# Key and block compression of the last mixer beside the feed-forward ahead of it, and the last pair's splits in another order

## The chip, the cores and the metric

One core of a Trainium2 chip runs the whole network for one sequence of 256 tokens in one launch. The metric is the device time of the launch in microseconds (us); lower is better. Three runs of a kernel give a median and its spread, and one more execution is recorded by the hardware profiler.

## The reference

Two blocks of two layers each, in float32, with 1024 features. The first block has a gated linear recurrence, an attention with a position bias, and a SwiGLU feed-forward behind each. The second block has a short convolution, shared keys and values, and a sparse attention with three branches, between four SwiGLU feed-forwards. What matters here is the last mixer, cut to its core:

```
def _compress(x_raw, pos, w1, b1, w2):          # 15 overlapping blocks of 32 tokens
    blocks = x_raw[:, :, idx] + pos
    return jax.nn.gelu(flat(blocks) @ w1 + b1) @ w2

k_cmp = _rmsnorm(_compress(kv[0], ...), k_norm[0]);  v_cmp = _compress(kv[1], ...)
k_sel = _rmsnorm(kv[2], k_norm[1]);  k_win = _rmsnorm(kv[4], k_norm[2])

def _nsa(x, ...):                                # 16 heads of 64, 4 groups of keys
    q = _rmsnorm(proj[..., :1024], q_norm);  gate = sigmoid(proj[..., 1024:])
    p_cmp = softmax(q @ k_cmp / 8, valid) * valid
    out = gate0 * (p_cmp @ v_cmp) + gate1 * attend(q, k_sel, v_sel) + gate2 * attend(q, k_win, v_win)
    return out @ w_o

def _swiglu(x, w_gate_up, w_down):
    a, b = jnp.split(x @ w_gate_up, 2, axis=-1)
    return (jax.nn.silu(a) * b) @ w_down
```

With 256 tokens every block is selected and the window covers all keys, so both of the other branches are plain causal attention. The shared keys and values come from the state after `ffn3`; the queries come from the state after `ffn4`.

## The kernel before

The phases are hgrn, ffn0, moba, ffn1, final, ffn2, conv, ffn3, kv, ffn4, nsa, ffn5. Each engine's instructions are written out by hand in one function per phase and engine; semaphores join them. Every weight is streamed in chunks of 1 MB (128 partitions x 2048 floats) through three buffers `raw` (`RING`). A float32 product of full accuracy is made of three fast ones: ACT copies the chunk to a rounded high part `whi`, DVE subtracts to get the low part `wlo` (both are called a split, `split`, L668 and L1200), and PE adds high x high, low x high and high x low.

SP issues the loads in the order of `Chunks.plan`. A load into a buffer waits until the chunk that held it, three earlier, was split by both engines; a chunk that is used unsplit (`direct`, the four `w1` of the compression) frees its buffer only when PE has multiplied with it.

A feed-forward (`ffn`) goes over 11 pairs of 256 hidden columns. For pair i there is a gate chunk g, an up chunk u and a down chunk d. PE's order per stage is g(i+1), then d(i), then u(i+1) (`across_pair` L1831 and L1833, `down_part` L1946). DVE's order is split g(i+1), `sum_gate(i)`, split d(i), `multiply(i)` (L1269, L1271), `low_part(i)` (L1286), split u(i+1); ACT has split g, `activate`, split d, `up_low` (L750), `high_part` (L756), split u. PE waits for `hlo_ready` of pair i before d(i). The last pair is made in two halves: `last_multiply`, `last_low` (L1282) on DVE, and `down_last` on PE, which adds the last down chunk first for token tile 0, then for tile 1. DVE's `add` (L1295) puts the sums into h, a root on GpSimd and `normalise` (L1222) follow, and PE's `turn` (L1889) transposes the result for the next phase.

The last mixer (`nsa`) does the following before its attention, in PE's order: projection of queries (two halves x two tiles, `along` L1848, L1849, L1854), gates (L2264, L2265), transposes of the normalised keys (L2280), compression with four direct chunks (L2293), key output (L2303), transposes of the queries (L2313), scores against the compressed keys (L2323), value output (L2330), 16 filler matmuls that compute nothing (`keep_warm` L1882), transposes of the compressed probabilities (L2337). DVE makes the squares and scales of keys and queries; the inverse roots come from GpSimd (`pow`, L1154).

Its attention handles 16 units: 8 pairs of heads, two branches each. For unit i, PE makes masked scores (L2120, L2124), DVE their maxima (L1490) and a scaling of these four values (L1494), ACT the exponentials with sums (L931), DVE the normalised probabilities (L1500 to L1508), PE the transposes (L2134), ACT the copy of these to SBUF (L939), PE the product with the values (L2356 with the compressed values, L2361 with the others), ACT and DVE the high and low part of the result once a pair (L944 `y_high`, L1513 `y_low`). Three of the four `out` chunks are split before the attention, the fourth after.

## Time and profile before

| | us |
|---|---|
| median of 3 runs | 1676.4 |
| lowest, highest | 1675.95, 1678.55 |
| profiled execution, its own time | 1678.77 |
| span of the profiled execution | 1677.0 |
| PE busy | 1653.9 |
| DVE busy | 1019.3 |
| ACT busy | 791.2 |
| mean granted TensorE clock | 0.995 |

The span runs from the first to the last instruction of the profiled execution. Busy times are sums per engine over the span; matmuls overlap in the array, so an engine at 99% may still hold short gaps between the starts of its instructions. The clock is a share of the full 2.4 GHz.

### The profile page before, as it was taken

What the parts mean: (1) busy time and instruction counts of PE and PEld (TensorE: products, weight loads), DVE (VectorE), ACT (ScalarE), POOL (GpSimd) and SP (SyncE); (2) the same over time, 40 slices, a digit from 0 to 9 for tenths busy, and PEclk for the clock granted to TensorE, in tenths of its full rate; (3) what the DMA queues carried; (4) which work ended last, traced back from release to release, by engine and by line L of the source; (5) the groups of instructions that cost most, each with busy time, mean ns of one, the idle gap of its engine ahead of it and who ended that gap; (6) DMA issues with size and microseconds to landing.
All of it is one profiled execution on the core that took longest, in us unless ns stands there. A gap on an engine that the chain in (4) does not pass through costs nothing.

```text
span 1677.0 us, 22634 instructions
## 1 busy us (share of the span) xinstructions
PE 1653.9 (99%) x9525; PEld 1425.5 (85%) x9525; DVE 1019.3 (61%) x1067; ACT 791.2 (47%) x954; POOL 61.3 (4%) x73
## 2 busy tenths in 40 slices
PE   9999999999999999999999999999999999899999
PEld 7998888889888887888898888888888886688887
DVE  6676655575565657555675655565555676765555
ACT  5333544455454445444443444455444435744443
POOL 0123000000000001000000000000000020000000
PEclk9999999999999999999999999999999998999999
DMA  8534567565355565555565456557555543045562
GB/s 276 171 126 134 188 188 219 196 196 165 129 181 191 175 209 172 200 193 191 185 214 174 167 175 201 175 189 238 184 192 191 166 145 132 1 142 187 175 209 90
DMA packets 221110, 294.82 MB, mean 176 GB/s; under 512 B 7516, under 2 KB 184880, under 8 KB 221010
## 3 DMA queue, kind: packets, MB, share of 16 engines
q1 hardware_dynamic: 215546, 284.40, 51.3%
q10 hardware_dynamic: 5464, 9.00, 2.1%
q8 instruction: 75, 1.23, 0.3%
q14 instruction: 25, 0.20, 0.0%
HBM read 290.75 MB, written 1.57 MB: 174 GB/s over the span
## 4 chain that ended last, share of the span: by engine, by line
PE 85%; DVE 8%; ACT 4%; issue 2%; DMA 0%; POOL 0%; SPq 0%; ACTq 0%; DVEq 0%; POOLq 0%
PE ps L1831 24%; PE ps L1946 18%; PE ps L1833 12%; PE ps L1822 3%; PE ps L1819 3%; PE ps L1820 3%; PE ps L1848 3%; PE ps L1854 3%; PE ps L1849 3%; DVE wlo L1200 3%; ACT whi L668 2%; PE ps L1898 1%; PE ps L1900 1%; PE ps L1899 1%; PE ps L2042 1%
## 5 line engine op out<-in xcount | busy, mean ns | idle before, releaser
L1200 DVE TENSOR_TENSOR wlo<-raw,whi 128x2048 fp32r<-128x2048 f32 (+2 forms) x270 | 601.8, 2248 | 302.1 <-ACT whi L668 300.8
L668 ACT ACTIVATE whi<-raw 128x2048 fp32r<-128x2048 f32 (+1 forms) x265 | 498.1, 1901 | 64.1 <-PE ps L1822 17.9
L1831 PE MATMUL ps<-x_both,whi 128*128 128x512 f32 x1920 | 480.3, 392 | 0.0
L1831 PEld LDWEIGHTS ps<-x_both,whi 128*128 128x128 f32 x1920 | 348.6, 189 | 64.8
L1833 PEld LDWEIGHTS ps<-x_both,wlo 128*128 128x128 f32 x1920 | 261.9, 190 | 18.7
L1833 PE MATMUL ps<-x_both,wlo 128*128 128x256 f32 x1920 | 267.7, 282 | 0.0
L1946 PE MATMUL ps<-whi,hhi 128*128 128x512 f32 x480 | 187.6, 391 | 0.0
L1946 PE MATMUL ps<-wlo,hhi 128*128 128x512 f32 x480 | 187.5, 391 | 0.0
L1946 PE MATMUL ps<-whi,hlo 128*128 128x512 f32 x480 | 186.7, 389 | 0.0
L750 ACT ACTIVATE hid<-ps 128x512 f32<-128x512 f32 x54 | 32.3, 598 | 224.9 <-PE ps L1833 224.9
L1819 PE MATMUL ps<-x_both,whi 128*128 128x256 f32 x512 | 127.7, 287 | 0.0
L1820 PE MATMUL ps<-x_both,wlo 128*128 128x256 f32 x512 | 125.5, 283 | 0.0
L1269 DVE TENSOR_TENSOR hid<-ps,hid 128x512 f32<-128x512 f32 x54 | 37.3, 691 | 141.3 <-ACT hid L750 141.3
L744 ACT ACTIVATE silu<-silu 128x512 f32<-128x512 f32 x60 | 38.0, 634 | 150.6 <-DVE silu L1265 150.6
L1946 PEld LDWEIGHTS ps<-whi,hlo 128*128 128x128 f32 x480 | 90.1, 188 | 19.2
L1946 PEld LDWEIGHTS ps<-whi,hhi 128*128 128x128 f32 x480 | 90.3, 188 | 18.0 <-issue 0.9
L1946 PEld LDWEIGHTS ps<-wlo,hhi 128*128 128x128 f32 x480 | 90.4, 188 | 16.5
L1820 PEld LDWEIGHTS ps<-x_both,wlo 128*128 128x128 f32 x512 | 98.1, 192 | 0.2
L1819 PEld LDWEIGHTS ps<-x_both,whi 128*128 128x128 f32 x512 | 98.0, 191 | 0.2
L1848 PE MATMUL ps<-whi,x_both 128*128 128x512 f32 x232 | 90.9, 392 | 1.2 <-issue 0.9
L1849 PE MATMUL ps<-wlo,x_both 128*128 128x512 f32 x232 | 90.4, 390 | 0.0
L756 ACT ACTIVATE hhi<-hid 128x512 fp32r<-128x512 f32 x54 | 34.2, 634 | 101.2 <-DVE hid L1271 72.0
(245 smaller groups left out, 1709.5 us busy)
## 6 DMA issues: line engine op xcount, KB each, us to landing
raw<-in_ffn_w_gate_up SPq DMA_DIRECT2D x80, 1024.0 KB, 5.4
raw<-in_ffn_w SPq DMA_DIRECT2D x62, 1024.0 KB, 5.2
raw<-in_ffn_w_down SPq DMA_DIRECT2D x44, 1024.0 KB, 4.8
raw<-in_hgrn_w_in SPq DMA_DIRECT2D x16, 1024.0 KB, 5.9
raw<-in_moba_w_in SPq DMA_DIRECT2D x12, 1024.0 KB, 5.1
raw<-in_conv_w_in SPq DMA_DIRECT2D x10, 1024.0 KB, 5.6
raw<-in_ffn_w_gate_up SPq DMA_DIRECT2D x16, 512.0 KB, 5.1
raw<-in_kv_w SPq DMA_DIRECT2D x6, 1024.0 KB, 5.1
```

The lines of the kernel that those rows point to most:

```text
L668: act.activation(whi[s % WRING][:, 0:width], raw[n % RING][:, 0:width], ACT.Copy).then_inc(split_hi, 1)
L744: act.activation(silu[:], silu[:], ACT.Silu).then_inc(silu_ready, 1)
L1200: ins = dve.tensor_tensor(wlo[s % WRING][:, part], raw[n % RING][:, part], whi[s % WRING][:, part].bitcast(F32), ALU.subtract)
L1819: pe.matmul(out, hi[:, k, tile], xhi[:, k, :], start=k == 0, stop=False)
L1820: pe.matmul(out, lo[:, k, tile], xhi[:, k, :], start=False, stop=False)
L1822: mm = pe.matmul(out, hi[:, k, tile], xlo[:, k, :], start=False, stop=k == KT - 1)
L1831: pe.matmul(ps[:, bank + n, :], hi[:, k, tile], x_both[:, k], start=k == 0, stop=k == KT - 1, skip_group_check=True)
L1833: mm = pe.matmul(ps[:, bank + n, S:2 * S], lo[:, k, tile], xhi[:, k, :], start=False, stop=k == KT - 1, skip_group_check=True)
L1848: pe.matmul(out, xhi[:, k, tile], hi[:, k % 4, :], start=k == 0, stop=False)
L1849: pe.matmul(out, xhi[:, k, tile], lo[:, k % 4, :], start=False, stop=False)
L1854: mm = pe.matmul(out, xlo[:, k, tile], parts[k // 4][0][:, k % 4, :], start=False, stop=k == KT - 1)
L1946: mm = pe.matmul(out, a[:, k, tile], b[:, k, part], start=first and k == 0 and n == 0, stop=last and k == 1 and n == 2, skip_group_check=True)
```

## The change

Four parts; the line numbers of the changed kernel differ, so its rows are given by their own numbers.

1. *Keys and blocks in ffn4.* Everything that the mixer makes from the shared keys and values moves into `ffn4`: `keys_beside` on DVE, ACT and PE, called once a stage. Stage 1 holds gains and squares, 2 and 3 the scaling and duplication, 3 and 4 the key transposes on PE and their copies on ACT and the positions on DVE, 5 to 8 (`COMPRESS`) one compression chunk each. Each compression chunk is its own accumulation, added in SBUF by DVE (`compressed`). The factor 1/8 on the scores goes into the keys' gain, so L1494 and the `scale` of the exponentials are gone.
2. *The mixer in halves.* The compressed scores, their softmax and their transposes are made for heads 0 to 7 before the attention, for heads 8 to 15 inside it (`beside(i)`, `turn_cmp`, `keep_cmp`). Value output and the second half of the query transposes stand between the first two scores and the first transposes, in place of 12 fillers; the 16 fillers are gone too.
3. *Splits.* Before the attention DVE splits one `out` chunk and ACT two; the others come behind it.
4. *Feed-forward ends, all six.* DVE splits the last down chunk in two parts with product 0 between, and makes low part 0 before product 1. PE adds the high parts as soon as they are there, and waits for the low parts after that. The splits of the next phase's first chunk are halved around the adds.

```
@@ class Chunks, and SP's ffn
                 for i in range(2, PAIRS):
                     self.add(name, "g", i)
+                    if name == "ffn4" and i - 1 in COMPRESS:
+                        self.add("nsa", "w1", COMPRESS.index(i - 1), direct=True)
                     if i < PAIRS - 1:
                         self.add(name, "d", i - 1)
                     self.add(name, "u", i)
@@ PE, ffn
                     pe.wait_ge(hlo_ready, hids + i + 1)
+                    if name == "ffn4":
+                        keys_beside(i)
                     down(0, i)
...
+                        if name == "ffn4" and i in COMPRESS:
+                            pe.wait_ge(cz_kept, COMPRESS.index(i) + 1)
                         across_pair(6, name, "u", i + 1)
@@ PE, down_last, tile 0
                         for k in range(2):
+                            pe.wait_ge(hhi_ready, hids + PAIRS + k)
+                            for half in range(2):
+                                down_high(t, half, k, *parts)
                             pe.wait_ge(hlo_ready, hids + PAIRS + k)
                             for half in range(2):
-                                mm = down_part(t, half, k, *parts, high=xhi, low=xlo, last=True)
+                                mm = down_low(t, half, k, parts[0])
@@ DVE, ffn (ACT alike)
-                    split(name, "g", i + 1)
-                    sum_gate(i)
+                    if name == "ffn4" and i - 1 in COMPRESS:
+                        sum_gate(i)
+                        split(name, "g", i + 1)
+                    else:
+                        split(name, "g", i + 1)
+                        sum_gate(i)
...
                     multiply(i)
                     low_part(i)
+                    if name == "ffn4":
+                        keys_beside(i)
@@ DVE, maxima
-                if bias is None:
-                    link(ins)
-                    ins = dve.tensor_scalar(nmax[:, b, :], nmax[:, b, :], scale, None, ALU.mult)
                 ins.then_inc(max_ready, 1)
@@ PE, nsa
+                along(2, 0, name, "q", between=first_turns)
...
+                pe.wait_ge(nq_ready, 2)
+                pe.wait_ge(kct_ready, 2)
+                cmp_scores(0)
                 along(3, 1, name, "q")
+                pe.wait_ge(gates_ready, 1)
+                pe.wait_ge(cmp_probs, 1)
...
+                def second():
+                    pe.wait_ge(gelu_ready, 2)
...
+                    turn_q(2, 6)
+                    pe.wait_ge(cl_kept, 1)
+                    turn_q(3, 7)
+                def beside(i):
+                    if i == 1:
+                        pe.wait_ge(cpt_ready, 1)
+                        pe.wait_ge(vc_kept, 1)
+                    if i == 2:
+                        pe.wait_ge(nq_ready, 4)
+                        pe.wait_ge(pt_ready, at.att + 1)
+                        cmp_scores(1)
@@ ACT, nsa, before the attention
+                cmp_exps(0)
+                split(name, "out", 0)
+                split(name, "out", 1)
                 keep(3)
@@ DVE, nsa
+                def beside(i):
+                    if i == 0:
+                        q_scale(3)
+                    if i == 1:
+                        dve.wait_ge(cmp_done, 2)
+                        dve.tensor_copy(vc[:], ...).then_inc(vc_kept, 1)
+                    if i == 2:
+                        cmp_logits(1)
+                    if i == 3:
+                        cmp_shift(1)
+                    if i == 5:
+                        cmp_sum(1)
+                    if i == 6:
+                        cmp_scale(1)
...
+                q_squares(0)
+                split(name, "q", 0)
+                split(name, "q", 1)
+                q_scale(0)
+                q_squares(1)
+                dve.wait_ge(gelu_ready, 2)
+                link(dve.memset(cp[:], 0.0))
+                q_scale(1)
...
+                split(name, "out", 0)
+                q_squares(3)
                 attention(...)
+                split(name, "out", 1)
+                split(name, "out", 2)
                 split(name, "out", 3)
```

What stands in a row on an engine now, at three places. First SP's queue of loads in ffn4, from gate chunk 6 on, before and then changed (`in_cmp_w_2` is the compression weight):

```order
127 L525 DMA raw<-in_ffn_w_gate_up 128x8x256 x2
128 L525 DMA raw<-in_ffn_w_down 128x2x1024
129 L525 DMA raw<-in_ffn_w_gate_up 128x8x256 x2
130 L525 DMA raw<-in_ffn_w_down 128x2x1024
131 L525 DMA raw<-in_ffn_w_gate_up 128x8x256 x2
```

```order
127 L528 DMA raw<-in_ffn_w_gate_up 128x8x256 x2
128 L528 DMA raw<-in_cmp_w_2 128x8x256
129 L528 DMA raw<-in_ffn_w_down 128x2x1024
130 L528 DMA raw<-in_ffn_w_gate_up 128x8x256 x2
131 L528 DMA raw<-in_cmp_w_2 128x8x256
132 L528 DMA raw<-in_ffn_w_down 128x2x1024
```

A compression chunk now stands between a gate and a down chunk. The gate chunk after next takes the buffer of a compression chunk.

Next DVE's queue in ffn4 for stage 6, changed: the compression's sum (L1322), gelu's argument (L1328 to L1330), the split of u7, `sum_gate(7)` (L1375), the splits of g8 and d7, and stage 7's product and low part.

```order
565 L1322 TENSOR_TENSOR arena<-ps,arena 128x60 x2
566 L1328 TENSOR_TENSOR arena<-arena 128x120
567 L1329 TENSOR_SCALAR arena<-arena 128x120
568 L1330 TENSOR_TENSOR arena<-arena 128x120
569 L1238 TENSOR_TENSOR wlo<-raw,whi 128x2048
570 L1375 TENSOR_TENSOR silu<-ps,silu 128x512
571 L1238 TENSOR_TENSOR wlo<-raw,whi 128x2048 x2
572 L1379 TENSOR_TENSOR hid<-ps,hid 128x512
573 L1381 TENSOR_TENSOR hid<-hid,silu 128x512
574 L1396 TENSOR_TENSOR hlo<-hid,hhi 128x512
```

Before, the sum of the gate stood behind the split of the gate chunk, and nothing of the compression stood here.

Last PE's queue around the start of the attention, before (L1882 are fillers) and then changed (L2467 transposes of the first half's probabilities, L2475 value output, L2436 the second half of the query transposes):

```order
3687 L2323 MATMUL ps<-arena 128x30 x16
3688 L2330 MATMUL ps<-w2sb,junk 128x64 x8
3689 L1882 MATMUL ps<-zero 128x512 x16
3690 L2337 MATMUL ps<-const,arena 128x128 x8
3691 L2120 MATMUL ps<-mask_b,ident_b 128x384 x2
...
3697 L1882 MATMUL ps<-zero 128x512 x12
```

```order
3697 L2467 MATMUL ps<-const,arena 128x128 x4
3698 L2260 MATMUL ps<-mask_b,ident_b 128x384 x2
...
3704 L2475 MATMUL ps<-w2sb,junk 128x64 x8
3705 L2436 MATMUL ps<-const,xn 128x128 x8
3706 L2260 MATMUL ps<-mask_b,ident_b 128x384 x2
```

Both groups of fillers are gone; the value output and eight query transposes stand where the second group stood.

## Rows read from the trace of the kernel before

**Rows 1.** The page: busy time of the engines, and ACT's split in its groups

```profile
PE 1653.9 (99%) x9525; PEld 1425.5 (85%) x9525; DVE 1019.3 (61%) x1067; ACT 791.2 (47%) x954; POOL 61.3 (4%) x73
...
L668 ACT ACTIVATE whi<-raw 128x2048 fp32r<-128x2048 f32 (+1 forms) x265 | 498.1, 1901 | 64.1 <-PE ps L1822 17.9
```

**Rows 2.** Timeline, end of ffn4: start, duration, engine, line, count, wait before

```profile
1329.80 2.29 DVE L1200 TENSOR_TENSOR wlo<-raw,whi 128x2048 fp32r<-128x2048 f32 x1 [2.50 <-ACT whi L668]
...
1333.34 0.39 PE L1946 MATMUL ps<-whi,hlo 128*128 128x512 f32 x1
...
1334.16 0.47 PE L1946 MATMUL ps<-whi,x_both 128*128 128x512 f32 x1 [0.43 <-DVE x_both L1282]
...
1337.84 1.28 DVE L1295 SCALAR_TENSOR_TENSOR h<-ps,h 128x512 f32<-128x512 f32 x2
...
1341.53 0.39 PE L1946 MATMUL ps<-whi,x_both 128*128 128x512 f32 x1
...
1341.98 1.32 PE L1889 MATMUL ps<-const,xn 128*128 128x128 f32 x8
...
1348.15 1.03 PE L1889 MATMUL ps<-const,xn 128*128 128x128 f32 x8
```

**Rows 3.** ffn4: timeline of a stage, two loads' us to landing, a busy stretch's windows

```profile
1254.02 0.69 DVE L1269 TENSOR_TENSOR hid<-ps,hid 128x512 f32<-128x512 f32 x1 [2.80 <-ACT hid L750]
...
1255.47 0.63 ACT L756 ACTIVATE hhi<-hid 128x512 fp32r<-128x512 f32 x1 [1.48 <-DVE hid L1271]
...
1243.69 2.57 SPq L525 DMA_DIRECT2D raw<-in_ffn_w_gate_up  x2
...
1260.31 2.57 SPq L525 DMA_DIRECT2D raw<-in_ffn_w_gate_up  x2
...
raw<-in_ffn_w_gate_up SPq DMA_DIRECT2D x1, 1024.0 KB, 5.3
...
raw<-in_ffn_w_gate_up SPq DMA_DIRECT2D x1, 1024.0 KB, 6.3
...
1246.00:1251.00 5.00, 5.00 (x27) 4.29 (x27) 2.50 (x2) 2.44 (x2) 0.00 (x0) 1.00 1.09 360
```

**Rows 4.** Mixer before its attention: PE's line L2293, timeline, GpSimd's line, windows (PEclk, DMA, GB/s last)

```profile
L2293 PE MATMUL ps<-arena,raw x128: 275/275/320, 1372.3 to 1387.0; 128*128 128x60 f32 x128
...
1391.44 6.92 PE L2323 MATMUL ps<-arena 128*128 128x30 f32 x32 [2.20 <-ACT arena L1098]
1398.17 3.65 PE L2330 MATMUL ps<-w2sb,junk 128*128 128x64 f32 x16
1401.62 5.38 PE L1882 MATMUL ps<-zero 128*128 128x512 bf16 x16
...
L1154 POOL TENSOR_TENSOR qrs<-qss,const x4: 1943/2036/2224, 1366.1 to 1377.0; 128x8 f32<-128x8 f32 x4
...
1391.50:1405.10 13.60, 13.60 (x57) 11.39 (x58) 10.96 (x13) 7.22 (x5) 0.00 (x0) 0.50 0.65 213
```

**Rows 5.** Attention: PE's timeline, and line L1494 (min/median/max ns, first and last start)

```profile
1408.61 0.50 PE L2120 MATMUL ps<-mask_b,ident_b 128*128 128x384 bf16 x2 [0.74 <-ACT arena L1105]
...
1415.06 0.87 PE L2134 MATMUL ps<-const,arena 128*128 128x128 f32 x6
...
1425.01 0.88 PE L2134 MATMUL ps<-const,arena 128*128 128x128 f32 x6 [0.34 <-DVE arena L1508]
...
L1494 DVE TENSOR_SCALAR nmax<-nmax x16: 170/170/172, 1411.1 to 1458.8; 128x4 f32<-128x4 f32 x16
```

**Rows 6.** Timeline of SP and DVE ahead of and right behind the attention

```profile
1397.83 3.70 SPq L522 DMA_DIRECT2D raw<-in_ffn_w_gate_up  x4
...
1466.76 0.42 DVE L1513 TENSOR_TENSOR x_both<-ps,x_both 128x256 fp32r<-128x256 f32 x1 [3.47 <-ACT x_both L944]
```

**Rows 7.** Windows around two other long waits of PE: us, busy times, PEclk, DMA, GB/s

```profile
440.40:446.00 5.60, 3.16 (x12) 2.67 (x11) 3.10 (x7) 2.02 (x3) 0.00 (x0) 0.70 0.51 161
911.80:918.00 6.20, 4.11 (x18) 3.27 (x18) 6.10 (x7) 3.03 (x4) 0.00 (x0) 1.00 1.02 321
```

More of the change, by code:

```diff
@@ L1303, in ffn @@
                 for i in range(1, PAIRS - 1):
-                    split(name, "g", i + 1)
-                    sum_gate(i)
+                    if name == "ffn4" and i - 1 in COMPRESS:
+                        sum_gate(i)
+                        split(name, "g", i + 1)
+                    else:
+                        split(name, "g", i + 1)
+                        sum_gate(i)
                     if i == 1:
@@ L1320, in ffn @@
                 sum_gate(PAIRS - 1)
-                split(name, "d", PAIRS - 1)
+                split(name, "d", PAIRS - 1, parts=(0,))
                 after = FOLLOWS.get(name)
                 last_multiply(0)
+                split(name, "d", PAIRS - 1, parts=(1,))
+                last_low(0)
                 last_multiply(1)
-                last_low(0)
                 last_low(1)
-                if after:
-                    split(after, "first", 0)
                 if not after:
-                    add(0)
-                    add(1)
+                    for t in range(TT):
+                        for half in range(2):
+                            add(t, half)
                     return
+                split(after, "first", 0, parts=(0,))
+                for half in range(2):
+                    add(0, half)
+                split(after, "first", 0, parts=(1,))
                 split(after, "first", 1, parts=(0,))
-                add(0)
+                normalise("final" if name == "ffn1" else after, 0)
+                add(1, 0)
                 split(after, "first", 1, parts=(1,))
-                normalise("final" if name == "ffn1" else after, 0)
-                add(1)
+                add(1, 1)
                 if name == "ffn1":
@@ L1513, in y_low, with attention @@
                 dve.tensor_tensor(dst, src, high.bitcast(F32), ALU.subtract).then_inc(ylo_ready, 1)
-            def attention(pairs, branches, pair_out, scale, gate):
+            def attention(pairs, branches, pair_out, gate, beside):
                 units = pairs * branches
@@ L1759, in nsa @@
+                q_squares(3)
+                attention(NH // 2, 2, nsa_out,
+                          lambda u: gates[:].rearrange("p t (h b) -> p t h b", b=3)[:, :, 2 * (u // 2):2 * (u // 2) + 2, 1 + u % 2], beside)
+                split(name, "out", 1)
+                split(name, "out", 2)
                 split(name, "out", 3)
@@ L2142, in values, with attention @@
                 pv(u, att_pt[:, u % 2]).then_inc(pv_done, 1)
-            def attention(pairs, branches, q_of, k_of, pv, warm):
+            def attention(pairs, branches, q_of, k_of, pv, second, beside):
                 units = pairs * branches
@@ L2259, in nsa @@
                 along(0, 0, name, "first", between=lambda: turn(name, 1))
+                pe.wait_ge(gelu_ready, 1)
+                for k in range(2):
+                    mm = pe.matmul(ps[0:NG * N_CMP, 2, 0:HD], cz[:, k * NG * N_CMP:(k + 1) * NG * N_CMP], w2sb[:, k, :], start=k == 0, stop=k == 1)
+                mm.then_inc(cmp_done, 1)
                 along(1, 1, name, "first")
@@ L2365, in nsa @@
                 pe.wait_ge(zero_ready, 4)
-                attention(NH // 2, 2, q_of, k_of, pv, warm=WARM_NSA)
+                pe.wait_ge(q_kept, 4)
+                attention(NH // 2, 2, q_of, k_of, pv, second, beside)
                 out_product(name, pieces=8)
```

482 lines of the change are left out of this document (265 added, 217 removed).

## The prediction

> **What bounds the kernel now.** I read the page's busy times first, then PE's timeline in the four places that the change touches, and last the queues behind each wait found there. TensorE (PE) is busy for 99% of the span [rows 1]. So a gain is only matmul work dropped, a wait of PE removed, or matmuls at a higher clock; work of ScalarE (ACT), VectorE (DVE) or a DMA counts only where it makes PE wait.
>
> - *Ends of the six feed-forwards* [rows 2]: PE meets the last pair's low half too early. Its starts stand at 1333.34 and 1334.16, 0.82 apart instead of the usual 0.23: 0.59 us lost, six times. The transposes for the next stage start 0.45 after the matmul ahead (again 0.23 is usual) and take 1.32 instead of 1.03: 0.51 lost.
> - *Inside ffn4* [rows 3]: no wait of PE shows. A stage (gate, down and up chunk) repeats every 16.62 us (SP's issues at 1243.69 and 1260.31). The down chunk is 24 matmuls 0.227 apart, 5.4 us; gate and up have 5.6 each.
> - *The last mixer before attention* [rows 4]: PE waits 2.20 us for ACT, and in the 13.6 us from 1391.5 the granted clock is 0.50, the 1.2 GHz level. There the 16 scores take 6.7 us by their starts, the value output 3.4, the 16 fillers 5.2 (5.38 less the overlap with what follows).
> - *Attention* [rows 5]: 16 units from 1411.1 to 1458.8, 6.4 us a pair of heads. The loop that closes is y_low, maxima, L1494, exponentials, transposes, exponentials again, y_high. PE is nearly as full: it waits 0.34 a pair.
>
> **The change, part by part.** A gain has a minus.
>
> *A. Feed-forward ends.* High parts now start on `hhi_ready`, and DVE makes low part 0 before product 1. DVE in ffn4 from 1329.80: half a split (1.15) to 1331.0, product 0 to 1331.9, the other half to 1333.1, low 0 to 1333.5, low 1 at 1335.2. PE wants the high part at 1333.6, low 0 at 1334.5 and low 1 at 1335.8. No wait is left: 6 x 0.59 = 3.5. The two adds end at 1337.7 instead of 1339.1 [rows 2], so the first normalised half is there at 1340.8 and PE, now due at 1341.1, needn't wait: 4 x 0.51 = 2.0 (ffn0, 2, 3, 4; ffn1 has fillers and the final norm there, ffn5 no follower, both costed at nothing). **A = -5.5**; -3 if one DVE result is late after all, -6 with ffn1.
>
> *B. Work into ffn4.* 16 transposes (2.0 us, two sets of 8 at 1.03) and 128 passes of compression (1372.3 to 1387.0 [rows 4], with 0.4 of the key output between: 14.3, or 3.6 a chunk) leave the mixer and reappear in ffn4: zero by themselves, as PE is the bound in both. What is new lies in the queues. DVE's added 4 us a stage at most fit its idle time: three splits of 2.29 and four steps of 0.69 are 9.6 us in 16.6. But the ring has three buffers, and a compression chunk is freed by PE's matmuls, not by the splits. Count in stages 6, 7 and 8 from PE's start on a gate chunk: compression ends at 5.6 + 3.6 = 9.2. Only then are the next gate, compression and down chunk loaded in a row. A chunk by itself lands 5.3 us after its issue; the second of a pair, issued 2.20 later, lands after 6.3, so 3.2 behind the first [rows 3]. The down chunk lands at 9.3 + 5.3 + 2 x 3.2 = 21.0. In ACT's and DVE's order its splits stand ahead of the up chunk's products: 1.9 + 2.3 + 0.7 + 0.7 + 0.65 + 0.7 = 7.0 [rows 1 to 3], low part at 28.0. PE wants it one stage (5.6 + 3.6 + 5.4 + 5.6 = 20.2) and 5.6 on, at 25.8. It waits 2.2, three times; the wait shifts the freeing by the same amount, so it stays 2.2. Stage 5 gives 0.4 by the same count. **B = +7.0**. Bounds: at 360 GB/s, the busiest five microseconds, a chunk follows after 2.9, wait 1.6, +5; if the first chunk too takes 6.3, the wait is 3.2, +10. I take 3.2 between chunks, the spacing of a real pair.
>
> By the Trainium skill (DMA: Bandwidth & Descriptors, Bandwidth) a very long stream moves at 425 GB/s. That would put 2.5 us between chunks and B near +3; the five microseconds at 360 don't reach it.
>
> *C. The mixer before attention.* Beside what moved (B) these go: the waits 2.2 and 0.7 [rows 4, 5]; the fillers 5.2; the value output 3.4 (it now stands where PE had 12 fillers); half the scores (3.35), and half the time of the rest, at twice the clock (1.7); half of the query and probability transposes (1.0 + 0.5). That is 18.05. Two waits are new. GpSimd's power takes 1.94 to 2.2 us [rows 4], and q_squares(1) now comes behind two splits on DVE: by the durations the second query transposes come 1.1 late. ACT reaches keep(3) after two more splits, and attention waits 0.9 for that. **C = -16.0**; bounds -13 (clock low for the scores, 1.3 more of waits) and -18 (no new wait).
>
> *D. Attention.* From the first scores to the first transposes it took 6.45 (1408.61 to 1415.06 [rows 5]). Now come both scores, value output, two sets of query transposes (one behind maxima(0), the power and q_scale(3)) and DVE's copy of vc: 8.2 by the same durations, +1.75. At i = 2 PE makes 8 scores (1.7), DVE waits for them ahead of maxima(3), and PE for DVE ahead of its transposes: +2.1. ACT's two copies for the compressed probabilities (0.4 each) and DVE's scaling at i = 6 (1.0) don't hide fully: +1.3. Without L1494 (0.17, with its link 0.24) the loop is shorter in the last 3.5 pairs: -0.85. **D = +4.3**, bounds +1 (nearly all beside the loop) and +7.
>
> *E. After attention.* Three of DVE's splits now come behind it. The first load of ffn5, before at 1397.83, is issued when out chunk 1 is split, 2.3 after 1467.2 [rows 6]. It lands near 1475, the second chunk near 1480, their splits end at some 1484.5; PE's sums of token tile 0 are ready 72 matmuls after about 1466, at 1482.4. About half of the 2 us is hidden behind tile 1: **E = +0.8**, bounds 0 and 2.
>
> Sum: -5.5 + 7.0 - 16.0 + 4.3 + 0.8 = **-9.4 us**. The profiled execution took 1678.8 (span 1677.0), 2.4 above the median of 1676.4. Taken from the median: **1667.0 us**.
>
> **The rivals.** A measurement of this kernel tells 0.2%, 3.4 us, from no change.
>
> *R1, the chunks come in time.* If the down chunk lands by 18.8 there is no wait, B is 0, and the time 1660.0. For it: the engines reach 360 GB/s. Against: three chunks in the 9.5 us from their issue would be 331 GB/s with no delay at the start, and a chunk's 5.3 us hold about 2 of delay. Chance 0.2.
>
> *R2, the clock falls in the new waits, and the result is slower.* Three waits of PE of over 2 us stand in the trace. After the 2.20 us before 1391.44 the clock was 0.50 for 13.6 us [rows 4]. Around 441 (PE busy 3.16 of 5.60) the mean clock is 0.70, so 3.4 us at 0.50; around 913 (busy 4.11 of 6.20) it stays 1.00 [rows 7]. My three waits of 2.2 in ffn4 are like them. PE's work takes twice as long at 1.2 GHz: three falls of 3.4 us cost 3 x 1.7 = 5.1 (1672.1), three of 13.6 cost 20.4, time 1687.4, slower than before. It decides from 9.4 us of cost on: three falls of over 6.3 us each. Against the long form: around 1391 the matmuls are small (128x30), in ffn4 dense ones follow. Short falls 0.15, a slower kernel 0.07.
>
> The Trainium skill (TensorE: Matmul & The Clock Gate, HAM oscillation) speaks against this change in the same way: a loop that waits for a DMA in each round can fall back to half clock in each round. By that rule all three waits would fall; the trace has two falls in three waits, and agrees in part.
>
> *R3, the ends are bound elsewhere.* If PE's wait for the low half only moves on to the next DVE result, A is 0 and the time 1672.5. The 1 us and more between DVE's results and PE's demand speaks against it. 0.05.
>
> **How the numbers follow.** The forecast's own case 0.5 (1660 to 1675 by the bounds, rarely all on one side), R1 0.2, R2 0.15 and 0.07, R3 0.05, other 0.03. The range leaves out the slow form of R2 and little else: 1657 to 1675. Slower by over 0.2% is R2's long form: 0.06. Within 0.2% (1673 to 1679.8) takes the upper edge of the forecast and of R2's short form: 0.06. Faster 0.88.
>
> **What would show it.** No wait `ps <- x_both L1282` at feed-forward ends (A). In ffn4 three PE waits near 2.2 us for DVE's low part ahead of the 128x60 matmuls, and SP's loads in bursts of three right after these (B). Clock 1.00 up to attention's first scores, waits of 1 us at a query transpose and ahead of the first scores (C). Longer first pairs, later ones near 6.3 us (D). PE waits of over 3 us in ffn4, or a granted clock of 0.50 there, would prove the forecast wrong.

## The result and the profile after

The changed kernel takes **1669.6 us** (median of 6 runs, 1668.2 to 1672.4), the kernel before beside it 1677.9 (6 runs, 1675.95 to 1680.05). The ratio is 0.9948, 95% interval 0.9938 to 0.9958: 8.7 us less, between 7.0 and 10.4. The forecast was 9.4 us less and a time of 1667.0, in a range of 1657 to 1675. The profiled execution of the changed kernel took 1668.95 (span 1667.1).

The page's busy times stand to [rows 1] as follows.

```profile
PE 1645.2 (99%) x9497; PEld 1420.7 (85%) x9497; DVE 1017.7 (61%) x1076; ACT 793.6 (48%) x958; POOL 69.0 (4%) x73
```

DVE and ACT have the work of before. PE lost 8.7 us of busy time, almost all of the difference, and GpSimd is busy for more time with as many instructions: that turns out to be a cause.

To see where the time went I took the start of each phase's first projection matmul from the timeline (us from the span's start) and the steps between them. Of ffn4's 22.6, 16.3 is work moved in. Its end saved only 0.2: from the last pair's first product with a low half to tile 1, thirteen starts took 3.66 us before, 2.95 after at the five other ends, and 3.31 here, and the turn wait grew by 0.2. So A is 2.3 in sum and B is 22.6 - 16.3 + 0.2 = 6.5. The span starts with 1.2 us less before any changed work. That stretch takes 165.6 to 168.4 in the 13 profiled executions of this document, so it is no effect of the change. Moba takes 0.2 more.

| step | before | after | difference | what it holds |
|---|---|---|---|---|
| ffn0, ffn2, ffn3 | 187.18, 186.07, 185.97 | 186.66, 185.54, 185.47 | -0.52, -0.53, -0.50 | term A |
| ffn1 | 189.01 | 189.14 | +0.13 | term A, with 0.9 more of waiting |
| ffn5 | 187.92 | 187.25 | -0.67 | term A |
| conv | 96.16 | 97.73 | +1.57 | nothing of the change |
| ffn4 | 185.05 | 207.69 | +22.64 | A, B, and 16.3 moved in |
| nsa to the first scores | 64.77 | 31.18 | -33.59 | C, and 16.3 moved out |
| attention | 57.61 | 59.76 | +2.15 | term D |
| behind it, to ffn5 | 22.83 | 23.41 | +0.58 | term E |

**End of ffn4, after** (timeline; the last column is the idle time before a row and what ended it), beside [rows 2]:

```profile
1355.44 0.50 PE L2073 MATMUL ps<-whi,x_both 128*128 128x512 f32 x1
...
1357.02 0.19 PEld L2073 LDWEIGHTS ps<-whi,x_both 128*128 128x128 f32 x1 [0.33 <-ACT x_both L786]
...
1358.48 1.29 DVE L1404 SCALAR_TENSOR_TENSOR h<-ps,h 128x512 f32<-128x512 f32 x2
...
1359.69 2.35 DVE L1238 TENSOR_TENSOR wlo<-raw,whi 128x1024 fp32r<-128x1024 f32 x2
...
1360.72 1.41 POOL L1172 TENSOR_SCALAR ms<-ss 128x1 f32<-128x1 f32 x1 [164.05 <-ACT xn L696]
...
1362.88 1.41 DVE L1260 SCALAR_TENSOR_TENSOR xn<-h,rstd,gain 128x512 f32<-128x512 f32 x2 [0.84 <-POOL rstd L1174]
1363.69 1.32 PE L1987 MATMUL ps<-const,xn 128*128 128x128 f32 x8 [0.26 <-DVE xn L1260]
```

The gap of 0.82 ahead of the last pair is gone; four short ones, for the last split and ACT's high part, are left of it, 0.36 in sum. The wait ahead of the transposes is not: 1363.69 follows 0.65 behind the matmul ahead (1363.04), where 0.23 is usual and before it was 0.45. Two half splits of DVE, one behind the other (2.35), stand between the adds and the normalisation, and GpSimd's first step of the root lasts 1.41 us beside them. Before, the same step was short:

```profile
1340.06 0.36 POOL L1136 TENSOR_SCALAR ms<-ss 128x1 f32<-128x1 f32 x1 [214.46 <-ACT xn L692]
```

**Stage 7 of ffn4, after**: timeline, loads of the burst behind the compression (KB, us from issue to landing), and two windows (PEclk, DMA share and GB/s last), beside [rows 3]:

```profile
1296.35 1.92 ACT L672 ACTIVATE whi<-raw 128x2048 fp32r<-128x2048 f32 x1 [3.99 <-DMA raw<-in_ffn_w_down]
...
1298.30 2.29 DVE L1238 TENSOR_TENSOR wlo<-raw,whi 128x2048 fp32r<-128x2048 f32 x1 [3.61 <-ACT whi L672]
...
1300.51 0.69 DVE L1379 TENSOR_TENSOR hid<-ps,hid 128x512 f32<-128x512 f32 x1
1301.23 0.69 DVE L1381 TENSOR_TENSOR hid<-hid,silu 128x512 f32<-128x512 f32 x1
1301.96 0.63 ACT L774 ACTIVATE hhi<-hid 128x512 fp32r<-128x512 f32 x1 [3.21 <-DVE hid L1381]
...
1302.62 0.69 DVE L1396 TENSOR_TENSOR hlo<-hid,hhi 128x512 fp32r<-128x512 f32 x1 [0.70 <-ACT hhi L774]
1303.37 5.26 PE L2041 MATMUL ps<-arena,raw 128*128 128x60 f32 x32 [1.50 <-DVE hlo L1396]
```

```profile
raw<-in_ffn_w_gate_up SPq DMA_DIRECT2D x1, 1024.0 KB, 5.2
...
raw<-in_cmp_w SPq DMA_DIRECT2D x1, 1024.0 KB, 7.7
...
raw<-in_ffn_w_down SPq DMA_DIRECT2D x1, 1024.0 KB, 7.6
...
1303.40:1312.30 8.90, 8.90 (x41) 8.10 (x42) 3.36 (x4) 4.56 (x6) 0.00 (x0) 0.62 0.27 89
1281.40:1290.30 8.90, 8.90 (x55) 8.00 (x56) 3.94 (x7) 2.14 (x3) 0.00 (x0) 1.00 0.46 148
```

The chain is the forecast one. The down chunk lands at 1296.3, its two splits and the products follow, and the low part lets PE go 7.0 us later, at 1303.37. PE's idle times ahead of the four compressions are 0.21 (1259.94), 1.00 (1281.40), 1.50 (1303.37) and none (1326.88). Then the clock falls: 0.50 for 6.8 us from 1305.4, and the same 8.9 us hold 41 matmuls where the stage before has 55.

**Mixer and attention, after**: window of the mixer, PE's waits, GpSimd's power (min/median/max ns), and the transposes of two late pairs, beside [rows 4, 5]:

```profile
1365.50:1396.70 31.20, 30.52 (x164) 24.97 (x164) 23.70 (x43) 17.78 (x27) 8.31 (x6) 1.00 0.39 135
...
1386.31 0.66 PE L2436 MATMUL ps<-const,xn 128*128 128x128 f32 x4 [0.24 <-DVE xn L1768]
...
1396.73 0.48 PE L2260 MATMUL ps<-mask_b,ident_b 128*128 128x384 bf16 x2 [0.46 <-ACT xn L1093]
...
1404.01 0.84 PE L2274 MATMUL ps<-const,arena 128*128 128x128 f32 x6 [0.66 <-DVE arena L1813]
...
L1190 POOL TENSOR_TENSOR qrs<-qss,const x4: 1635/1641/3556, 1376.7 to 1399.0; 128x8 f32<-128x8 f32 x4
...
1435.41 0.87 PE L2274 MATMUL ps<-const,arena 128*128 128x128 f32 x6 [0.25 <-DVE arena L1624]
...
1441.78 0.88 PE L2274 MATMUL ps<-const,arena 128*128 128x128 f32 x6
```

The clock is 1.00 in all of the mixer, and its new waits are 0.24 and 0.46, or 0.4 and 0.6 by the spacing of starts (predicted 1.1 and 0.9). A late pair takes 6.37 instead of 6.58. Ahead of ffn5's first product stands one more wait, 0.84 between starts for 0.23; it is all of the +0.58 behind the attention:

```profile
1471.05 2.29 DVE L1238 TENSOR_TENSOR wlo<-raw,whi 128x2048 fp32r<-128x2048 f32 x1 [1.67 <-ACT whi L672]
1473.26 1.28 DVE L1276 TENSOR_TENSOR h<-ps,h 128x512 f32<-128x512 f32 x2
...
1479.22 1.07 ACT L702 ACTIVATE x_both<-ps 128x512 fp32r<-128x512 f32 x2
...
1479.90 0.47 PE L1946 MATMUL ps<-whi,x_both 128*128 128x512 f32 x1 [0.44 <-issue]
```

The profile calls it "issue", but PE starts 0.1 us behind the end of ACT's first copy (1479.8), which stands at the end of a chain from DVE's split over the adds.

### The profile page after: what moved, and what is told of

Read it like the earlier page. It is cut to its first block, busy times and chain, and to the rows that moved or that the text cites. A ratio compares the mean times of both kernels' runs of the same rounds, so it can differ in the third digit from the quotient of the medians.

```text
span 1667.1 us, 22598 instructions
## 1 busy us (share of the span) xinstructions
PE 1645.2 (99%) x9497; PEld 1420.7 (85%) x9497; DVE 1017.7 (61%) x1076; ACT 793.6 (48%) x958; POOL 69.0 (4%) x73
## 3 DMA queue, kind: packets, MB, share of 16 engines
HBM read 290.75 MB, written 1.57 MB: 175 GB/s over the span
## 4 chain that ended last, share of the span: by engine, by line
PE 86%; DVE 7%; ACT 3%; DMA 2%; issue 1%; POOL 1%; SPq 0%; DVEq 0%; POOLq 0%; ACTq 0%
PE ps L1929 24%; PE ps L2066 18%; PE ps L1931 13%; PE ps L1917 3%; PE ps L1920 3%; PE ps L1918 3%; PE ps L1946 3%; PE ps L1952 3%; PE ps L1947 3%; DVE wlo L1238 2%; PE ps L1996 2%; PE ps L1997 1%; PE ps L1998 1%; PE ps L2182 1%; ACT whi L672 1%
## 5 line engine op out<-in xcount | busy, mean ns | idle before, releaser
L2066 PEld LDWEIGHTS ps<-wlo,hhi 128*128 128x128 f32 x480 | 90.8, 189 | 16.6
```

What stands on the lines that cost most here:

```text
L2066: mm = pe.matmul(out, a[:, k, tile], b[:, k, part], start=first and k == 0 and n == 0, stop=last and k == 1 and n == 2, skip_group_check=True)
```

## The experiments

Eleven further kernels were run, 4 to 11 times each. All ratios are against runs of the kernel before on the same chip; us are worked out from the ratio at 1677.9. Steps and waits are those of one profiled execution per kernel.

| run | ratio, 95% interval | us less than before |
|---|---|---|
| the change | 0.9948, 0.9938 to 0.9958 | 8.7 |
| ends alone | 0.9989, 0.9981 to 0.9998 | 1.8 |
| ends undone | 0.9975, 0.9963 to 0.9986 | 4.2 |
| one half split | 0.9951, 0.9939 to 0.9963 | 8.2 |
| ends spread | 1.0101, 1.0087 to 1.0115 | -16.9 |
| products first | 0.9909, 0.9896 to 0.9922 | 15.3 |
| fillers in ffn4 | 0.9934, 0.9922 to 0.9947 | 11.1 |
| before without fillers | 1.0000, 0.9991 to 1.0009 | 0.0 |
| scaling back | 0.9964, 0.9952 to 0.9976 | 6.0 |
| products and fillers | 0.9894, 0.9881 to 0.9908 | 17.8 |
| products and ends | 0.9897, 0.9883 to 0.9911 | 17.3 |
| products, fillers and ends | 0.9880, 0.9867 to 0.9894 | 20.1 |

### 1. What the ends are worth: alone, and undone

The kernel before with part 4 of the change (DVE shown; PE's `down_last` as in the change):

```
-                split(name, "d", PAIRS - 1)
+                split(name, "d", PAIRS - 1, parts=(0,))
                 last_multiply(0)
-                last_multiply(1)
+                split(name, "d", PAIRS - 1, parts=(1,))
                 last_low(0)
+                last_multiply(1)
                 last_low(1)
-                split(after, "first", 0)
-                split(after, "first", 1, parts=(0,))
+                split(after, "first", 0, parts=(0,))
                 add(0)
+                split(after, "first", 0, parts=(1,))
+                split(after, "first", 1, parts=(0,))
-                split(after, "first", 1, parts=(1,))
                 normalise("final" if name == "ffn1" else after, 0)
-                add(1)
+                add(1, 0)
+                split(after, "first", 1, parts=(1,))
+                add(1, 1)
```

> The kernel before with part 4 of the change alone (the feed-forward ends). As predicted (term A): all low-half waits and turn waits gone, 5.5 us less than before. By the trace of the changed kernel: the low-half wait of 0.59 goes, but the wait ahead of the next stage's transposes stays near 0.4 to 0.6 because GpSimd's first root step takes 1.4 us while DVE works on half splits (0.36 before): each of five ends saves 0.5 to 0.7, ffn1's nothing, 2.6 us less than before. If the ends are bound elsewhere altogether: no change.

The interval is 0.3 to 3.2 us less: 5.5 is outside, 2.6 inside. Its own steps give -0.51, +0.12, -0.53, -0.54, -0.52 and -0.73 for the six feed-forwards, 2.7 in sum. GpSimd's step is 1.41 in it too.

The reverse, the changed kernel with the ends of before (the same lines with + and - exchanged):

> The changed kernel with the ends of before (parts 1 to 3 alone). If the ends are worth 2.6 us: 6 us less than before, 2.6 more than the changed kernel; if they are worth the predicted 5.5: 3 us less than before, 5.5 more than the changed kernel. The steps from the start of ffn4 to the start of ffn5 should be those of the changed kernel but for one end (0.5 us): about 8 us less than before in sum.

2.3 to 6.2 us less than before: the times can't tell the two theories apart here, both lie inside. The steps can: all feed-forwards but ffn4 are back at their old times within 0.06 us, ffn4 takes 208.48 (0.8 more than in the changed kernel, as the gap of 0.82 at its end is 1.52 here), the mixer 113.73. Together with the first run, term A is about half of what I booked.

### 2. GpSimd's step beside DVE's split: one half split

```
                 split(after, "first", 0, parts=(1,))
-                split(after, "first", 1, parts=(0,))
                 normalise("final" if name == "ffn1" else after, 0)
+                split(after, "first", 1, parts=(0,))
                 add(1, 0)
                 split(after, "first", 1, parts=(1,))
                 add(1, 1)
```

> The changed kernel with one half split instead of two between the adds and the normalisation at each feed-forward end; the second half comes behind the normalisation. If GpSimd is slowed by the DVE split beside it: its first root step falls from 1.4 us to 0.4 to 0.6, the transposes' wait of 0.4 to 0.6 goes at ffn0, 2, 3 and 4, and ffn1's wait of 1.2 shrinks: 2 to 3 us less than the changed kernel. If GpSimd's 1.4 us are its own (the first instruction after a long idle time, whatever DVE does): no change.

In time this is a miss: the same as the changed kernel. In the trace the mechanism is there. Timeline at the end of ffn4:

```profile
1359.79 1.22 DVE L1238 TENSOR_TENSOR wlo<-raw,whi 128x1024 fp32r<-128x1024 f32 x1
1360.82 0.36 POOL L1172 TENSOR_SCALAR ms<-ss 128x1 f32<-128x1 f32 x1 [164.46 <-ACT xn L696]
...
1363.38 1.03 PE L1987 MATMUL ps<-const,xn 128*128 128x128 f32 x8
...
1369.61 1.32 PE L1987 MATMUL ps<-const,xn 128*128 128x128 f32 x8 [0.19 <-DVE xn L1260]
```

With one half split beside it GpSimd's step takes 0.36, again ending 0.1 to 0.2 us behind DVE's split, and the first transposes wait no more. So the 1.41 are not GpSimd's own. The steps of ffn0, 1, 2 and 3 are 0.68, 0.35, 0.51 and 0.74 shorter. But the second half split now stands ahead of token tile 1's last add, and that tile's transposes (1369.61) wait instead: conv takes 0.71 and the shared keys 0.65 more. The gain moved one stage on and was spent there.

### 3. Later still: ends spread

```
                 add(1, 0)
-                split(after, "first", 1, parts=(1,))
+                split(after, "first", 1, parts=(0,))
                 add(1, 1)
...
                 normalise(after, 1)
+                split(after, "first", 1, parts=(1,))
                 x_low(after, 1)
```

> As the run with one half split before the normalisation, but the adds of token tile 1 keep their place behind it: one half split before each of the normalisation and the last add, the last half split behind tile 1's normalisation. With one half split GpSimd's step already took 0.36 us, but the gain came back as a loss in the next stage (conv 0.7, shared keys 0.65 us longer). If that loss is tile 1's add standing behind a half split: ffn0, 2, 3 and 4 each take 0.5 us less than in the changed kernel and the stages behind them no more; 2 to 2.5 us less in all. If DVE as a whole is short of time there: no change against the changed kernel.

I had taken the last half split as not wanted before tile 1. It is, by tile 0:

```profile
1392.31 0.76 PE L1946 MATMUL ps<-whi,x_both 128*128 128x512 f32 x1 [3.60 <-DVE wlo L1238]
```

PE uses the second half of the first chunks 1.6 us into the next phase. It waited 3.6 us for the split, and the transposes of tile 1 stand behind that wait in PE's order. Such a wait stands behind five ends, ffn0 to ffn4, and the clock falls beside each. The kernel is slower than before by 1%.

### 4. Late chunks in ffn4: products first

ACT's order is changed in the same way (`up_low` and `high_part` ahead of the down chunk's split):

```
@@ DVE, ffn
+                    early = name == "ffn4" and i in COMPRESS
+                    if early:
+                        multiply(i)
+                        low_part(i)
                     if i < PAIRS - 2:
                         split(name, "d", i)
...
-                    multiply(i)
-                    low_part(i)
+                    if not early:
+                        multiply(i)
+                        low_part(i)
```

> The changed kernel with ACT's and DVE's products and low part of pairs 5 to 8 in ffn4 ahead of the down chunk's split. If the waits of PE ahead of the compression are the down chunk's late landing, handed on by the order of the splits: the waits of 0.4, 1.0 and 1.5 us vanish, the down chunk has 4.8 us to spare behind the compression, the clock does not fall at 1305, and ffn4 takes 6.5 us less. If the clock falls there whatever PE waits: 3 us less. If something else (the up chunk, DVE's own time) takes the place of the wait: no change.

The window of ffn4's second half, here and then in the changed kernel:

```profile
1258.00:1350.00 92.00, 92.00 (x543) 81.26 (x542) 50.34 (x52) 44.05 (x41) 0.00 (x0) 1.00 0.61 206
```

```profile
1258.00:1350.00 92.00, 89.29 (x509) 78.62 (x508) 45.32 (x48) 37.84 (x35) 0.00 (x0) 0.96 0.57 195
```

In this window PE is busy all the time at full clock, and the step of ffn4 takes 201.05 instead of 207.69: 6.64 less, 6.5 expected; in time 6.6 (15.3 against 8.7). The chunks land as late as before (the down chunk of stage 7 at 1296.1, 11.3 behind the end of the compression). Only the products no longer stand behind a split that nobody wants yet.

### 5. The clock and the idle time: fillers in ffn4

```
@@ PE, ffn
+                    if name == "ffn4" and i in (6, 7, 8):
+                        for _ in range(5):
+                            pe.matmul(ps[:, 0, :], zero[:, 0:P], zero[:], start=False, stop=False, skip_group_check=True)
                     pe.wait_ge(hlo_ready, hids + i + 1)
```

> The changed kernel with five matmuls that add zeros (1.15 us) ahead of PE's wait in stages 6, 7 and 8 of ffn4. The late chunks stay, only PE's idle time is filled. If the idle time is what lets the clock fall: the granted clock stays 1.00 from 930 to the end of ffn4, stage 7's compression and down chunk run at full speed, 3.4 us less there, but stage 8 now waits (1 us or is filled by its five): 2 to 3 us less than the changed kernel. If the clock falls for another reason: the same 0.50 for 6.8 us near 1305, and no change or 1 us more.

```profile
1303.00:1313.00 10.00, 9.34 (x62) 7.81 (x61) 5.36 (x8) 5.78 (x6) 0.00 (x0) 1.00 0.22 71
1409.30:1412.70 3.40, 3.40 (x22) 2.38 (x20) 2.67 (x10) 0.98 (x3) 0.00 (x0) 0.50 0.01 2
```

The chunks are as late, and PE still starts the compression only with the low part, but its clock stays at 1.00 through ffn4. That step takes 206.03, 1.7 less; the other half of the fall's 3.4 went into stage 7, where PE waits 0.66 behind its fillers (1.15), and into stage 8, where the slow clock had hidden the late chunk and PE now spends the five fillers (1.15) and 0.2 of waiting. In time the kernel is 2.4 us below the changed one, as expected, though the two intervals overlap. A new fall of 3.4 us stands at 1409, in attention, where the changed kernel's trace has none; the mixer's step is 1.0 longer with it.

### 6. What the mixer's fillers cost: before without fillers

```
-WARM_NSA = (12, 0)
-WARM_CMP = 16
+WARM_NSA = (0, 0)
+WARM_CMP = 0
```

> The kernel before without its 16 and 12 filler matmuls. The prediction booked the 16 fillers (5.2 us) as time that the change gives back. If they bounded the mixer: 5 us less. If the softmax of the compressed scores on DVE and ACT is what PE waits for, they only fill its time: no less, PE idle for about 5 us in their place, and the clock no higher than before in the first attention units, so the same or 1 to 3 us more. In that case the gain is due to the softmax chain no longer standing in PE's way, not to the fillers gone.

Timeline and window (ending in PEclk, DMA share, GB/s) of this kernel, then the same window of the kernel before:

```profile
1406.50 1.97 PE L2337 MATMUL ps<-const,arena 128*128 128x128 f32 x8 [5.84 <-DVE arena L1752]
...
1395.00:1415.00 20.00, 12.25 (x60) 9.13 (x59) 13.87 (x22) 8.29 (x15) 0.00 (x0) 0.57 0.49 158
```

```profile
1395.00:1415.00 20.00, 19.26 (x98) 12.60 (x98) 13.56 (x26) 8.14 (x22) 0.00 (x0) 0.75 0.48 158
```

No change in time. PE waits 5.84 us for the softmax of the compressed scores in the fillers' place. But the fillers were not free, as the timeline of the kernel before shows:

```profile
1393.26 6.70 DVE L1200 TENSOR_TENSOR wlo<-raw,whi 128x2048 fp32r<-128x2048 f32 x3 [3.48 <-ACT whi L668]
...
1399.87 0.72 DVE L1735 SCALAR_TENSOR_TENSOR arena<-ps,const 128x240 f32<-128x240 f32 x2
...
1404.64 0.73 DVE L1752 TENSOR_TENSOR arena<-arena,const 128x240 f32<-128x240 f32 x2
...
1406.84 1.04 PE L2337 MATMUL ps<-const,arena 128*128 128x128 f32 x8
```

The softmax was finished at 1405.4 and PE went on with fillers: the transposes started 15.40 us behind the first score, without fillers 13.66. So 1.7 of the 5.2 us were on the path. Without fillers the clock stayed at 0.50 for 17.1 us instead of 13.7, the transposes took 1.97 instead of 1.04, and the first unit of the attention 6.94 instead of 6.45. From the mixer's start to ffn5 0.4 us of the 1.7 were left. In the trace of the ends alone the low clock lasted only 10.2 us, the same 16 fillers took 4.51 us, and the transposes came 13.74 behind the first score.

The softmax itself began when DVE had done its three splits of `out` chunks, 8.43 us behind the first score in both kernels, although the 32 scores took 6.92 us in one and 4.36 in the other. The change takes this chain out of PE's way by two edits at once: PE does the second half of the queries' projection beside the softmax of the first eight heads, and no `out` split stands ahead of that softmax on DVE. No run tells what each is worth.

### 7. The scaling in the attention loop: scaling back

```
@@ DVE, maxima
+                if bias is None:
+                    link(ins)
+                    ins = dve.tensor_scalar(nmax[:, b, :], nmax[:, b, :], 1.0, None, ALU.mult)
                 ins.then_inc(max_ready, 1)
```

> The changed kernel with a multiplication of the four negated maxima by one (0.17 us, 0.24 with its link) back in each of the 16 attention units. As predicted (term D): the loop is bound by DVE and ACT in the last 3.5 pairs only, 0.85 us more. If it is bound so in all eight pairs: 3.8 us more. If PE bounds it throughout: no change.

```profile
1445.57 0.88 PE L2277 MATMUL ps<-const,arena 128*128 128x128 f32 x6 [0.33 <-DVE arena L1627]
...
1452.14 0.88 PE L2277 MATMUL ps<-const,arena 128*128 128x128 f32 x6 [0.33 <-DVE arena L1627]
```

A pair takes 6.57 again, the time of before. The attention's step is 1.40 longer (61.16), seven times 0.2, spread from the first unit to the last pairs. It is between both theories: DVE and ACT bound the loop in nearly all pairs, but a pair holds two such multiplications and pays for one. The mixer as a whole is 1.93 longer (116.29); the other 0.5 is a chunk of ffn5 that landed 0.56 later in this execution, behind a burst of loads that the edit does not touch. In time it is 2.7 us, with overlapping intervals.

### 8. A better version: fillers, ends, and both

The run with the products first, and besides:

```
@@ PE, conv
-                keep_warm(6)
+                keep_warm(14)
@@ PE, moba
                 value(2)
+                for _ in range(9):
+                    pe.matmul(ps[:, 0, :], zero[:, 0:P], zero[:], start=False, stop=False, skip_group_check=True)
                 turn_probs(3)
```

> The run with the products first, and PE's two long waits in front of out products (2.6 us near 442, 2.25 us near 912) filled: 9 matmuls that add zeros in the first, 14 filler matmuls instead of 6 in the second. If idle time is what lets the clock fall: no granted clock of 0.50 near 442 and 912 in any run, 1.7 us less at each place where it fell, 3.4 us less than with the products alone, and a smaller spread between runs. If the clock falls anyway: no change.

```profile
441.00:447.00 6.00, 5.49 (x28) 4.26 (x27) 2.95 (x7) 2.62 (x2) 0.00 (x0) 1.00 0.59 178
911.00:917.00 6.00, 5.64 (x26) 4.45 (x25) 4.63 (x5) 2.40 (x2) 0.00 (x0) 1.00 0.85 286
```

Both falls are gone: the steps of moba (109.62 for 111.27) and conv (96.13 for 97.73) are 1.65 and 1.60 shorter. In time it is 2.5 us below the products alone (3.4 expected), with overlapping intervals; the runs spread over 1660.1 to 1662.2, with the products alone over 1661.0 to 1663.8.

The ends in a third order:

```
                 split(after, "first", 0, parts=(1,))
-                split(after, "first", 1, parts=(0,))
                 normalise("final" if name == "ffn1" else after, 0)
+                split(after, "first", 1, parts=(0,))
                 add(1, 0)
-                split(after, "first", 1, parts=(1,))
                 add(1, 1)
+                split(after, "first", 1, parts=(1,))
```

> The run with the products first, and at feed-forward ends one half split ahead of the normalisation, one behind it, then both adds of tile 1, the last half split after them. With the last add behind the last half split the gain of 0.6 us a stage end was lost again ahead of tile 1's transposes (0.35 and 0.17). Here that add is 1.1 us earlier, but the last half split ends 0.3 us after PE needs it (1.6 us into the next stage): 0.3 us less at each of four ends, 1.2 us less than the products alone. If that wait is as long as the one it replaces: no change.

```profile
1359.41 0.47 PE L1956 MATMUL ps<-whi,x_both 128*128 128x512 f32 x1 [0.20 <-DVE wlo L1243]
```

The wait for the last half split is there, 0.34 over the usual spacing (0.3 expected). The steps of ffn0 to ffn4 are 3.2 us shorter in sum; moba, conv, the shared keys and the mixer give back 1.5 once moba's clock, which did not fall in this execution, is set aside. That leaves 1.7, in time 2.0 with overlapping intervals.

> Both edits of the two other runs together: 4.6 us less than the products alone if both hold, about 1657.5 us.

1658.7 us (median of 4 runs, 1658.4 to 1659.1), 20.1 less than before and 11.4 less than the change. It is 4.8 less than the products alone, 4.6 expected. Its trace still has one fall of the clock, 3.4 us at 1397.5, and 1.4 us more of attention with it.

## Why the prediction was right, and where its terms were off

The time was inside the range, 2.6 above the forecast in its own runs (1669.6 for 1667.0); by the ratio the gain was 8.7 for 9.4. The terms were off by more than the sum, so part of the match is luck:

| term | predicted | from the steps |
|---|---|---|
| A ends | -5.5 | -2.3 |
| B ffn4 | +7.0 | +6.5 |
| C mixer before attention | -16.0 | -17.3 |
| D attention | +4.3 | +2.2 |
| E behind it | +0.8 | +0.6 |
| conv (clock at 912), moba, start of the program | 0 | +0.5 |
| sum | -9.4 | -9.8 |

**A failed in its second half.** The low-half wait went as foreseen at five ends, where it proved worth 0.71, and by half at ffn4's (0.36): 3.9 for the 3.5 booked. The step that failed is "the first normalised half is there at 1340.8 and PE, now due at 1341.1, needn't wait: 4 x 0.51 = 2.0". I moved the adds forward and carried the path behind them over unchanged, though the same edit puts a second half split beside GpSimd's root. That root took 1.41 for 0.36 (runs 1 and 2), and the turn wait grew by 0.2 at four ends; at ffn1, which I had at nothing, it grew from 0.34 to 1.21, more than the saving there. A was -2.3, outside the bound of -3 that I had given, and I had given that bound for "one DVE result late": the mechanism wasn't on my list, and R3, with 0.05, was nearest to it.

**B's sum was right, its parts were not.** The queue argument held: the waits are the down chunk's landing, handed on by the split order, as products first shows. One number was mis-sized. I put 3.2 us between the chunks of a burst; they came 2.5 to 3.0 apart. The down chunk landed 10.6 (stage 6) and 11.15 (stage 7) behind the end of the compression, not 11.7, so the waits were 1.0 and 1.5 by the same formula (10.6 + 7.0 - 16.6 = 1.0), where I had 2.2 (11.7 + 7.0 - 16.6 is 2.1). The Trainium skill (DMA: Bandwidth & Descriptors, Bandwidth), which I had quoted for 2.5, was nearer in stage 6 and the row in stage 7. What filled the gap is R2 in its short form: a fall of 6.8 us, worth 3.4. That slower clock in turn hid stage 8's wait. Two errors of opposite sign, +3.4 for the clock and -4.3 for the waits (2.7 for my 7.0), made the sum look exact: that is luck. I had priced R2 on top of the waits, and it came in place of one of them.

**C was 1.3 better.** The new waits are 0.4 and 0.6 by the spacing of starts for my 1.1 and 0.9, 1.0 in all. GpSimd's power, 1.64 and not the 1.94 to 2.2 of [rows 4], is 0.3 to 0.6 of the first; the second, behind ACT's splits, does not pass through GpSimd. But the working gave a wrong reason for a right number. Of "the fillers 5.2" only 1.7 were a cost (run 6), and the low clock of the scores was none: the softmax waited for DVE's splits, not for them. What was saved is the stretch in which PE stood behind the splits and the softmax, and the parts added up only because each was one slice of that stretch. That stretch came from the order on DVE as well, which my working did not name.

**D was 2.1 better.** "Without L1494 ... the loop is shorter in the last 3.5 pairs: -0.85" was mis-sized: scaling back gave 1.4 in the attention, since nearly all pairs are bound by the loop. I had read 6.4 a pair from the first and the last start; the late pairs took 6.58. The first transposes came 7.3 behind the first scores, not 8.2, with GpSimd's faster power in that path as well. These two are 1.5 of the 2.1. Of the rest, unit 1 with its scores cost 1.9 for 2.1, and what I had as not hidden (+1.3) comes out at 0.85, if the 1.4 is taken as the gain.

**E was right in its path, and its size is a matter of landing times.** In all ten traces with the changed mixer DVE's adds start as the split of ffn5's second chunk ends. Where that split ends later than 16.3 us behind the attention's end, ffn5 starts 6.56 behind the end of the split, to 0.01: 16.42 and 22.97, 16.85 and 23.41 (the changed kernel), 17.41 and 23.96. The step of before is 22.83, so E came out between 0.0 and 1.1 with the same order of work, and 0.6 in the trace compared here. I had the splits end at 18.3 and half of the delay hidden.

**Clock.** That a wait of about 2 us may or may not cost clock was seen; its size was taken at one place only. At conv the same wait of 2.25 that kept 1.00 in [rows 7] cost 3.4 us at 0.50 in the changed kernel's trace, +1.57 in that step and unrelated to the change: the kernel before without fillers, whose conv is that of before, has the same fall and +1.61.

The rivals: R1 fell, since PE waited in ffn4; products first shows what it would have been worth. R2's long form fell too. Its short form is what happened in one of three places, for 6.8 us instead of 3.4.

## What to carry to other kernels

When an operand becomes ready early but its user stands behind an unrelated piece of work on the same engine, look at the order first: here the loads stayed as late as they were, and moving two products ahead of one split was worth 6.6 us. When an edit shortens a chain, re-time every link behind it with what the edit puts beside that link, on GpSimd above all. And before you book a filler's time as a gain, read when the operand behind it was ready: only what the filler runs over that moment is its cost, here 1.7 of 5.2 us.

## What the runs showed of the hardware

**GpSimd stands still beside DVE's split.** The root's first step (128x1) takes 0.30 us with DVE idle, or beside DVE operations that read PSUM. Begun during a split (SBUF and SBUF to SBUF) it ended 0.1 to 0.2 us behind the end of a split in every case: 0.36 long when one half split ended 0.19 behind its start, 1.41 when a second one followed at once. The power on 128x8 takes 1.64 in three of its four places in the changed kernel. It ended 1.45 to 1.51 us behind whatever DVE operation on two SBUF operands was running when it began: 3.56 beside a whole split, 1.94 to 2.22 beside operations of 0.7 to 1.0 us in the kernel before. One of 0.41 us that began 0.70 behind its start cost it nothing (1.64). The Trainium skill says it (Trainium Architecture — The Big Picture, What this means for kernel authors: "an exclusive lock (not a bandwidth split)"; GPSIMD Engine Reference, Specifications, names DVE instructions with two SBUF inputs), and the traces agree for what is running when GpSimd begins. GpSimd got no turn at a change of DVE instructions 0.19 us behind its start. It did at one 0.59 behind (0.76 at 652.60 in the kernel before, between two normalising steps), so that two in a row always shut it out is not shown.

**The same wait costs clock in some executions and not in others.** Eleven executions hold moba's wait of 2.6 us unfilled and eleven conv's of 2.25. At each place the clock fell in 8 of 11 (to 0.50, for 3.4 us, which costs about 1.6), and in none of the two where the wait was filled to 0.8 and 0.5. In ffn4 all five executions with unfilled waits ahead of the compression had falls of 6.8 us, and none of the five without them. In four the fall followed stage 7's wait (1.2 to 1.7) and not stage 6's (1.0 to 1.1); with the ends spread, stage 7 had no wait and falls followed stages 6 and 8, both 1.1. The Trainium skill (TensorE: Matmul & The Clock Gate, HAM oscillation) has a loop that waits for DMA fall back each time; its waits are 3 to 5 us, so the page does not say, as I had taken it, that waits of 2.2 would. Here it was some of the times, and after waits of 1.1 to 1.7 us too. Filled with matmuls that add zeros (ffn4, moba) or with plain fillers (conv), no such wait was followed by a fall. But in two of the ten executions with the changed mixer the clock fell 12 us into its attention (3.4 us at 1409 and 1397): fillers in ffn4, and products, fillers and ends. In the kernel before, the mixer's fillers ran at 0.50 themselves for 3.6 of their 5.2 us.
